# Attention values with the values stationary: two heads in the column halves, weights scaled before they are turned

## The chip, the cores and the metric

The kernel runs on one core of one Trainium2 chip. The metric is the device time of one execution, in microseconds; less is better. The engines are TensorE (PE in the rows; its weight loads are PEld), VectorE (DVE), ScalarE (ACT), GpSimd (POOL) and SyncE (SP), each with its own instruction queue, which it works off in order.

## What is computed

The reference is a small model of four layers on 512 tokens of width 1024, all in float32. Three of its layers hold an attention, and these are what the change is about. Cut to what matters:

```python
# layer 0, for each block of 128 queries, 8 heads of width 64 in 2 groups
o_cmp = masked_softmax(q @ kc.T * scale, cmask) @ vc      # 31 compressed keys
o_slc = masked_softmax(q @ ks.T * scale, smask) @ vs
o_win = masked_softmax(q @ kw.T * scale, wmask) @ vw
o = g0 * o_cmp + g1 * o_slc + g2 * o_win                  # gates per query and head
x = x + g_m * (concat(y_a, o) @ w_out)                    # y_a: a gated recurrence

# layer 1, 16 heads; every query keeps the keys that an index score picks
o = masked_softmax(q @ kg.T * scale, mask) @ vg
x = x + g_m * (o @ w_out)

# layer 3, 16 heads, a mask of dilated distances, rotary q and k
x = x + softmax(q @ k.T * scale + mask) @ v @ w_o
```

A row of weights is divided by its sum, and in layer 0 multiplied by its gate. That factor can be applied to the outputs (64 numbers a query and head) or to the weights (up to 512 a query and head); the result is the same.

## The kernel before

Activations lie turned: 128 features on the partitions, the 512 tokens along the row, eight such blocks for the width of 1024. A projection is worked off in "panels" of 128 output features. For each, SP loads 512 KB of raw weights, ACT rounds them to `w_hi` (L1160), POOL takes the difference `w_lo` (L578), and PE makes three matmuls a block, `three` (L606 to L609). Four panels are in flight (`RING`); POOL's work is nothing but these differences, in the order of the panels, and 26 additions in layer 2.

The three attentions (`attention(run, ...)`, one such function on PE, one on ACT, one on DVE, run = 0, 1, 2) share one scheme. The work is 32 pairs, and a pair is one block `i` of 128 queries with two heads `b` = 0, 1; its rows are `w = 128 * (i + 1)` keys wide. The order of the pairs is `PAIRS0` or `PAIRS1`: 16 pairs that alternate `i` = 3 and 0, then 16 that alternate `i` = 2 and 1. In what follows a **round** is two neighbouring pairs, so that an attention is 8 rounds of (3, 0) and 8 rounds of (2, 1). For pair `n`:

- PE `scores(n)`: two matmuls, one a head, of 64 rows each (L782), into the banks 0, 1 and 6 in turn;
- DVE `masked(n, b)`: adds the mask, writes the row to `prob` and its extreme to `stat` (L1732); `prob` holds two pairs;
- ACT: the exponential in place, and its sum (L1274);
- PE `turn(n)`: turns the rows, 128 columns a transpose (L792), into banks 2 and 3;
- ACT `copy_even(n)` (L1248) and DVE `copy_odd(n)` (L1742; for some pairs ACT, L1251) copy them to `probT`;
- PE `values(n)`: the turned weights are the stationary operand (128 by 128), 64 columns of values move; tokens come out on the partitions (L804), head `b` in columns `64 b`;
- DVE `invert(n)` (L1747) and `output(n)`: the reciprocal, in run 0 the gate (L1757), and the product into `orow` (L1764 in run 0, where it adds to what is there; L1767).

At the end blocks of `orow` are turned back to features on the partitions: PE `turn_out` (L817), ACT `out_high` (L1263) and DVE `out_low` (L1776), at hand-written places (`TURNED_AT`). `out_part` then makes the first two panels of the output projection, in two pieces.

The order on PE is `scores(n + 1)`, `turn(n)`, `values(n - 1)`; on DVE `masked(n, 0)`, `masked(n, 1)`, `copy_odd(n - 1)`, `invert(n - 1)`, `output(n - 2)`. Beside them DVE does other things: in run 0 `sum_in_steps` (24 steps, L1857 and L1860, on a 1 MB load each eight) and pieces of the recurrence, in run 1 `pick`, the choice of keys for the blocks still to come (L2154, L2156).

Two other places are touched. At the start, PE sums the squares of x over eight blocks (L861 to L865), and the norm of layer 0 waits for it (`invert_root(0)`, then `sum_first` and `first_h` on DVE, L1936 to L1944). Before the first attention, the compressed branch has its own values, `compressed_values` (L940) and `compressed_out` (L2054), which write `orow`.

## Time and profile before

| | us |
|---|---|
| median of 3 runs | 2536.79 |
| lowest, highest | 2529.05, 2537.76 |
| the profiled execution, its own time | 2536.1 |
| its span, first to last instruction | 2534.3 |
| PE, DVE, ACT, POOL busy in it | 2460.3, 1348.8, 935.5, 954.5 |
| mean granted TensorE clock | 0.981 |

Of the span, 1.8 us less than the execution's own time, PE is busy 97%. A busy PE is not a PE at its peak: matmuls are pipelined, and the duration of one record is longer than the time until the next can start. So steps are measured here from start to start. Times in rows are from the start of the span.

### The profile page before, as it was taken

What the parts mean: (1) busy time and instruction counts of PE and PEld (TensorE: products, weight loads), DVE (VectorE), ACT (ScalarE), POOL (GpSimd) and SP (SyncE); (2) the same over time, 40 slices, a digit from 0 to 9 for tenths busy, and PEclk for the clock granted to TensorE, in tenths of its full rate; (3) what the DMA queues carried; (4) which work ended last, traced back from release to release, by engine and by line L of the source; (5) the groups of instructions that cost most, each with busy time, mean ns of one, the idle gap of its engine ahead of it and who ended that gap; (6) DMA issues with size and microseconds to landing.
All of it is one profiled execution on the core that took longest, in us unless ns stands there. A gap on an engine that the chain in (4) does not pass through costs nothing.

```text
span 2534.3 us, 35767 instructions
## 1 busy us (share of the span) xinstructions
PE 2460.3 (97%) x12245; PEld 2025.4 (80%) x12245; DVE 1348.8 (53%) x2459; ACT 935.5 (37%) x1515; POOL 954.5 (38%) x409
## 2 busy tenths in 40 slices
PE   8999989999999899999999989999999999999998
PEld 7786778888877677888888768888888978888887
DVE  6777664443157765111117976545467465545445
ACT  3355433222233453322235444322246364432222
POOL 1320134444443103444444734444454402344443
PEclk9998999999999899999999999999999999999999
DMA  7540245554322102323323213333233201232322
GB/s 300 202 145 26 84 141 190 182 183 159 99 95 72 34 26 67 113 94 99 100 91 96 79 44 129 102 96 101 86 116 100 92 18 42 83 108 91 107 92 75
DMA packets 64344, 263.68 MB, mean 104 GB/s; under 512 B 7265, under 2 KB 7777, under 8 KB 57953
## 3 DMA queue, kind: packets, MB, share of 16 engines
q1 hardware_dynamic: 61056, 251.00, 29.9%
q10 hardware_dynamic: 3168, 11.08, 1.2%
q8 instruction: 76, 1.25, 0.2%
q14 instruction: 44, 0.35, 0.0%
HBM read 259.95 MB, written 2.10 MB: 103 GB/s over the span
## 4 chain that ended last, share of the span: by engine, by line
PE 85%; DVE 6%; issue 3%; ACT 2%; DMA 1%; DVEq 1%; POOLq 1%; POOL 1%; ACTq 0%; SPq 0%
PE bank L607 25%; PE bank L609 25%; PE bank L608 25%; PE bank L804 3%; PE bank L782 2%; PE bank L792 2%; DVE bank L1834 1%; DVE acc L1550 1%; DMA modraw<-in_pairs 1%; POOL w_lo L578 1%; POOLq L600 1%; DVE bank L2209 1%; PE bank L864 1%; PE bank L628 0%; PE bank L729 0%
## 5 line engine op out<-in xcount | busy, mean ns | idle before, releaser
L578 POOL TENSOR_TENSOR w_lo<-raw,w_hi 128x1024 fp32r<-128x1024 f32 x378 | 918.1, 2436 | 1548.2 <-ACT w_hi L1160 1546.8
L607 PE MATMUL bank<-h_hi,w_hi 128*128 128x512 f32 x1760 | 697.8, 396 | 12.6 <-DVE h_lo L1597 7.8
L608 PE MATMUL bank<-h_lo,w_hi 128*128 128x512 f32 x1760 | 690.3, 392 | 0.0
L609 PE MATMUL bank<-h_hi,w_lo 128*128 128x512 f32 x1760 | 690.1, 392 | 0.0
L1160 ACT ACTIVATE w_hi<-raw 128x1024 fp32r<-128x1024 f32 x378 | 392.6, 1051 | 472.9 <-PE bank L609 470.1
L607 PE MATMUL bank<-g_hi,w_hi 128*128 128x512 f32 x1072 | 418.6, 390 | 0.0
L609 PE MATMUL bank<-g_hi,w_lo 128*128 128x512 f32 x1072 | 417.2, 389 | 0.0
L608 PE MATMUL bank<-g_lo,w_hi 128*128 128x512 f32 x1072 | 417.1, 389 | 0.0
L607 PEld LDWEIGHTS bank<-h_hi,w_hi 128*128 128x128 f32 x1760 | 333.6, 190 | 89.9 <-DVE h_lo L1597 8.7
L609 PEld LDWEIGHTS bank<-h_hi,w_lo 128*128 128x128 f32 x1760 | 333.6, 190 | 71.2
L608 PEld LDWEIGHTS bank<-h_lo,w_hi 128*128 128x128 f32 x1760 | 333.9, 190 | 68.6 <-issue 0.5
L609 PEld LDWEIGHTS bank<-g_hi,w_lo 128*128 128x128 f32 x1072 | 201.2, 188 | 42.1
L608 PEld LDWEIGHTS bank<-g_lo,w_hi 128*128 128x128 f32 x1072 | 201.3, 188 | 41.5
L607 PEld LDWEIGHTS bank<-g_hi,w_hi 128*128 128x128 f32 x1072 | 201.3, 188 | 41.4
L1687 DVE TENSOR_TENSOR prod<-silu,bank 128x512 f32<-128x512 f32 x44 | 30.2, 687 | 299.8 <-PE bank L609 299.5
L1225 ACT ACTIVATE g_hi<-prod 128x512 f32 x66 | 41.7, 632 | 300.9 <-DVE prod L1687 197.3
L1613 DVE SCALAR_TENSOR_TENSOR x<-bank,plain,x 128x512 f32<-128x512 f32 x64 | 47.6, 749 | 153.7 <-PE bank L609 153.6
L1834 DVE SCALAR_TENSOR_TENSOR bank<-modraw,csil,bank 128x256 f32<-128x256 f32 x222 | 108.5, 489 | 17.2 <-issue 1.0
L1274 ACT ACTIVATE prob<-prob,stat 128x512 f32<-128x512 f32 (+1 forms) x192 | 105.6, 552 | 28.1 <-DVE stat L1732 28.0
L1613 DVE SCALAR_TENSOR_TENSOR x<-bank,modv,x 128x512 f32<-128x512 f32 x64 | 47.6, 749 | 112.1 <-PE bank L609 111.3
L1732 DVE CUSTOM_DVE_ANT_0 prob<-bank,mask 128x512 f32<-128x512 f32 (+1 forms) x192 | 86.4, 488 | 24.8 <-PE bank L782 21.5
L792 PEld LDWEIGHTS bank<-ident,prob 128*128 128x128 f32 x480 | 55.0, 149 | 51.7 <-ACT prob L1274 35.5
(300 smaller groups left out, 2685.8 us busy)
## 6 DMA issues: line engine op xcount, KB each, us to landing
raw<-in_panels SPq DMA_DIRECT2D x378, 512.0 KB, 3.5
modraw<-in_pairs SPq DMA_DIRECT2D x40, 1024.0 KB, 5.7
first_mods<-in_first SPq DMA_DIRECT2D x4, 2048.0 KB, 21.6
w<-in_w ACTq DMA_DIRECT2D x2, 2048.0 KB, 8.5
x<-in_x SPq DMA_DIRECT2D x1, 2048.0 KB, 8.6
out<-yout ACTq DMA_DIRECT2D x8, 256.0 KB, 2.2
mask<-in_causal ACTq DMA_DIRECT2D x1, 1024.0 KB, 4.8
mask<-in_dilated ACTq DMA_DIRECT2D x1, 1024.0 KB, 8.3
```

The source lines that it names most:

```text
L578: pool.tensor_tensor(w_lo[:, slot, :], raw[:, slot, :], w_hi[:, slot, :].bitcast(F32), ALU.subtract)\
L607: pe.matmul(out, w_h, m_h, start=start, stop=False)
L608: pe.matmul(out, w_h, m_l, start=False, stop=False)
L609: return pe.matmul(out, w_l, m_h, start=False, stop=stop)
L782: pe.matmul(bank[SBANK[(2 * n + b) % 3]][:, 0:w], q_of(run, pairs_[n], b), k_of(run, pairs_[n], b), start=True, stop=True).then_inc(score_ ...
L792: m = pe.transpose(bank[2 + b][:, P * j:P * j + P], prob[:, 2 * (n % 2) + b, P * j:P * j + P], ident[:, :])
L804: m = pe.matmul(bank[4 + n % 2][:, HD * b:HD * b + HD], probT[:, 2 * (n % 2) + b, P * j:P * j + P], v_of(run, pairs_[n], b, j), start=(j = ...
L1160: act.activation(w_hi[:, slot, :], raw[:, slot, :], ACT.Copy).then_inc(hi_ready, 1)
L1274: act.activation(row, row, ACT.Exp, bias=stat[:, 0, u % 64:u % 64 + 1], scale=-1.0, accum_out=stat[:, 1, u % 64:u % 64 + 1]).then_inc(exp_ ...
L1613: dve.scalar_tensor_tensor(out=x[:, n, :], in0=bank[p % RING][:, :], scalar=scale_by, in1=x[:, n, :], op0=MUL, op1=ADD).then_inc(bank_free, 1)
L1732: dve.tensor_tensor_reduce(prob[:, 2 * (n % 2) + b, 0:w], bank[SBANK[(2 * n + b) % 3]][:, 0:w], mask[:, i, 0:w], -SCALE, HIGHEST, ADD, ALU ...
L1834: m = dve.scalar_tensor_tensor(out=part if k < KB - 1 else to, in0=w[:, :, k, :], scalar=csil[:, k:k + 1], in1=part, op0=MUL, op1=ADD)
```

## The change

- **Values.** `values(n)` takes the values as the stationary operand (128 keys by 64 columns) and lets the turned weights move (128 tokens). The output is 64 features by 128 tokens, already the way the projection wants it; head 0 goes to partitions 0 to 63 and head 1 to 64 to 127 of the same bank, and the loop alternates the heads for each block of keys. The two pairs of a round, in run 0 four pairs (both branches), make a group that shares a bank, 4 or 5.
- **Scaling.** Tokens now lie along the row, so the factor of a token can't be applied to the outputs by a column. GpSimd multiplies the rows of weights by it, in place, before they are turned: 96 instructions on 128 by `2 w` elements. `turn(n)` waits for these (`weights_ready`), not for the exponentials.
- **Order.** The scores run three pairs ahead (`SCORES_AHEAD`), `prob` holds four pairs (`PROB_STEPS`), and the copies on ACT and DVE stand two steps later in their queues.
- **Gone.** `output`, `orow` and `turn_out`. `out_high` and `out_low` read a group's bank, 256 columns, 16 times in runs 1 and 2, 8 times in run 0. The first two output panels do seven of eight blocks before the last one.
- **Compressed branch.** Its probabilities are scaled by DVE (one instruction of 1024 columns), turned two panels later, and their values are two matmuls at the start of each group of run 0, in the same bank; `compressed_values` and `compressed_out` go.
- **Run 0's side work.** The sums for the modulation pause two steps after each eight (`STEP_AT`); the pieces `recurrence_low` go from DVE to POOL, between pairs 8 to 11.
- **Start.** POOL adds the squares two by two, so PE sums four blocks, not eight; `first_h(1)` stands before `sum_first(2)`, and PE does blocks 0 to 3 of the first panels ahead of `first_batch(2)`.

```diff
-        PAIRS0 = [(i, c, br) for both in TURNS for br in (1, 2) for c in range(4) for i in both]
+        PAIRS0 = [(i, c, br) for both in TURNS for c in range(4) for br in (1, 2) for i in both]
...
+        GROUP = (4, 2, 2)
...
         def odd_by_scalar(run, n):
-            return run == 0 and n % 2 == 1 or run == 1 and n < N_PAIR // 2
+            return run == 0 and n % 2 == 1 or run == 1 and n < N_PAIR // 2 and n % 2 == 0
...
         @block.gpsimd
+            def attention(run):
+                pairs_, at = (PAIRS0, PAIRS1, PAIRS1)[run], N_PAIR * run
+                for n in range(N_PAIR):
+                    w, u = P * (pairs_[n][0] + 1), 2 * (at + n) % 64
+                    both = prob[:, PROB_SLOT[n % PROB_STEPS], :, 0:w]
+                    pool.wait_ge(factor_ready, at + n + 1)
+                    pool.tensor_tensor(both, both, stat[:, 2, u:u + 2].rearrange("p (b o) -> p b o", o=1)
+                                       .broadcast_to((P, 2, w)), ALU.mult).then_inc(weights_ready, 1)
+                    if run == 0 and n in (8, 9, 10, 11):
+                        recurrence_low(n - 8)
...
+            for n in range(KB // 2):
+                pool.wait_ge(squares_ready, 2 * n + 2)
+                pool.tensor_tensor(sq0[:, 2 * n, :], sq0[:, 2 * n, :], sq0[:, 2 * n + 1, :], ALU.add).then_inc(two_added, 1)
+            split_from(0, P_OUT0 + RING)
+            attention(0)
...
         @block.tensor
                 def turn(n):
+                    pe.wait_ge(weights_ready, at + n + 1)
                     for b, copied in enumerate((pt_even, pt_odd)):
-                        pe.wait_ge(exp_ready, 2 * (at + n) + b + 1)
...
                 def values(n):
-                    if n >= 2:
-                        pe.wait_ge(o_done, at + n - 1)
...
-                            m = pe.matmul(bank[4 + n % 2][:, HD * b:HD * b + HD],
-                                          probT[:, 2 * (n % 2) + b, P * j:P * j + P], v_of(run, pairs_[n], b, j),
+                    if n % GROUP[run] == 0 and g >= 2:
+                        pe.wait_ge(ot_lo, OT_AT[run] + g - 1)
...
+                    for j in range(i + 1):
+                        for b in range(2):
+                            m = pe.matmul(out[rows_of(b), at_col:at_col + P], v_of(run, pairs_[n], b, j),
+                                          probT[:, 2 * (n % 2) + b, P * j:P * j + P], start=(run > 0 and j == 0),
...
                 for n in range(N_PAIR):
-                    if n + 1 < N_PAIR:
-                        scores(n + 1)
+                    if n + SCORES_AHEAD < N_PAIR:
+                        scores(n + SCORES_AHEAD)
                     turn(n)
                     if n:
                         values(n - 1)
...
         @block.scalar
                 for n, pair in enumerate(pairs_):
-                    if n:
-                        copy_even(n - 1)
+                    if n >= SCORES_AHEAD:
+                        copy_even(n - SCORES_AHEAD)
...
+                    if group_ended(run, n - SCORES_AHEAD - 1):
+                        out_high(n - SCORES_AHEAD - 1)
...
         @block.vector
                 for n in range(N_PAIR):
+                    masked(n, 0)
+                    if n >= SCORES_AHEAD and not odd_by_scalar(run, n - SCORES_AHEAD):
+                        copy_odd(n - SCORES_AHEAD)
+                    masked(n, 1)
                     if n:
                         invert(n - 1)
+                    if group_ended(run, n - SCORES_AHEAD - 1):
+                        out_low(n - SCORES_AHEAD - 1)
```

How this stands on the queues, at two places. First VectorE in the third attention, two neighbouring pairs of the first half. Before (the two ISA rows are `masked`, the numbers that follow are partitions by columns):

```order
L1732 ISA prob,stat<-bank,mask 128x128 [waits pt_done,score_ready]
L1732 ISA stat 128x1
L1732 ISA prob,stat<-bank,mask 128x128 [waits pt_done,score_ready]
L1732 ISA stat 128x1
L1742 COPY probT<-bank 128x512 [waits pv_done,pt_done]
L1747 RECIPROCAL stat<-stat 128x2 [waits exp_ready]
L1767 TENSOR_TENSOR orow_95<-bank,stat 128x128 [waits pv_done]
L1732 ISA prob,stat<-bank,mask 128x512 [waits pt_done,score_ready]
L1732 ISA stat 128x1
L1732 ISA prob,stat<-bank,mask 128x512 [waits pt_done,score_ready]
L1732 ISA stat 128x1
```

And now, the same two pairs' place in the queue:

```order
L1741 ISA prob,stat<-bank,mask 128x128 [waits pt_done,score_ready]
L1741 ISA stat 128x1
L1757 RECIPROCAL stat<-stat 128x2 [waits exp_ready]
L1769 TENSOR_TENSOR g_lo<-bank,g_hi 128x2x128 [waits ot_hi]
L1741 ISA prob,stat<-bank,mask 128x512 [waits pt_done,score_ready]
L1741 ISA stat 128x1
L1751 COPY probT<-bank 128x128 [waits pv_done,pt_done]
L1741 ISA prob,stat<-bank,mask 128x512 [waits pt_done,score_ready]
L1741 ISA stat 128x1
L1757 RECIPROCAL stat<-stat 128x2 [waits exp_ready]
L1741 ISA prob,stat<-bank,mask 128x128 [waits pt_done,score_ready]
L1741 ISA stat 128x1
```

The copy of a pair's odd head stood one step behind its `masked`; it stands three steps behind, between the two `masked` of a later pair, and the reciprocal of a pair comes after both `masked` of the next. The product into `orow` is gone.

Second TensorE in the same place. Before (L782 scores, L792 `turn`, L804 `values`):

```order
L792 MATMUL bank<-ident,prob 128x128 [waits pt_even,exp_ready]
L792 MATMUL bank<-ident,prob 128x128 [waits pt_odd,exp_ready]
L804 MATMUL bank<-v3t,probT 128x64 [waits pt_even,o_done]
L804 MATMUL bank<-v3t,probT 128x64 x3
L804 MATMUL bank<-v3t,probT 128x64 [waits pt_odd]
L804 MATMUL bank<-v3t,probT 128x64 x3
L782 MATMUL bank<-k_143,q_142 128x128 [waits masked_ready]
L782 MATMUL bank<-k_143,q_142 128x128
L792 MATMUL bank<-ident,prob 128x128 [waits pt_even,exp_ready]
L792 MATMUL bank<-ident,prob 128x128 x3
```

And now (L813 scores, L823 `turn`, L842 `values`):

```order
L823 MATMUL bank<-ident,prob 128x128 [waits pt_even,weights_ready]
L823 MATMUL bank<-ident,prob 128x128 [waits pt_odd]
L842 MATMUL bank<-probT,v3t 64x128 [waits pt_odd,pt_even]
L842 MATMUL bank<-probT,v3t 64x128 x7
L813 MATMUL bank<-k_141,q_140 128x128 [waits masked_ready]
L813 MATMUL bank<-k_141,q_140 128x128
L823 MATMUL bank<-ident,prob 128x128 [waits pt_even,weights_ready]
L823 MATMUL bank<-ident,prob 128x128 x3
L823 MATMUL bank<-ident,prob 128x128 [waits pt_odd]
L823 MATMUL bank<-ident,prob 128x128 x3
```

`turn` waits for `weights_ready`, which GpSimd gives, in the place of `exp_ready`; `values` needs one wait for both heads, and its rows have 128 moving columns and a 64-wide stationary operand.

## Rows read from the trace of the kernel before

**Rows 1.** The page: busy time, share of the span and instructions of TensorE.

```profile
PE 2460.3 (97%) x12245; PEld 2025.4 (80%) x12245; DVE 1348.8 (53%) x2459; ACT 935.5 (37%) x1515; POOL 954.5 (38%) x409
```

**Rows 2.** Windows: a stretch of the third attention, PE, PEld, DVE, ACT, POOL busy, clock.

```profile
2040.00:2070.00 30.00, 30.00 (x231) 23.92 (x230) 20.71 (x85) 18.94 (x62) 0.00 (x0) 1.00 0.01 2
```

**Rows 3.** Timeline: one round of the third attention's first half; start, us taken, engine, line.

```profile
2051.27 1.90 PE L804 MATMUL bank<-v3t,probT 128*128 128x64 f32 x16
...
2053.10 0.49 PE L782 MATMUL bank<-k,q 64*128 64x128 f32 x4
...
2053.52 1.09 PE L792 MATMUL bank<-ident,prob 128*128 128x128 f32 x8
...
2053.84 0.28 DVE L1732 CUSTOM_DVE_ANT_0 prob<-bank,mask 128x128 f32<-128x128 f32 x1
...
2054.65 0.69 DVE L1742 COPY probT<-bank 128x512 f32<-128x512 f32 x1 [0.52 <-PE bank L792]
...
2055.26 0.15 DVE L1747 RECIPROCAL stat<-stat 128x2 f32<-128x2 f32 x1
...
2056.27 1.90 PE L804 MATMUL bank<-v3t,probT 128*128 128x64 f32 x16
```

**Rows 4.** Timeline: one round of the third attention's second half.

```profile
2097.37 1.45 PE L804 MATMUL bank<-v3t,probT 128*128 128x64 f32 x12
...
2098.66 0.61 PE L817 MATMUL bank<-ident,orow 128*128 128x128 f32 x4
...
2102.81 1.45 PE L804 MATMUL bank<-v3t,probT 128*128 128x64 f32 x12
```

**Rows 5.** Timeline: matmuls whose stationary operand is 64 columns wide.

```profile
1464.61 1.09 PE L1097 MATMUL bank<-wsT,v2t 128*64 128x128 f32 x16
```

**Rows 6.** Groups and one line's durations (ns, min/median/max): GpSimd's tensor operations.

```profile
L578 POOL TENSOR_TENSOR w_lo<-raw,w_hi 128x1024 fp32r<-128x1024 f32 x378 | 918.1, 2436 | 1548.2 <-ACT w_hi L1160 1546.8 <-issue 1.1
L599 POOL TENSOR_TENSOR cout<-cout,tapped 128x512 f32<-128x512 f32 x26 | 35.1, 1351 | 5.1 <-issue 2.9 <-ACT tapped L1433 2.2
L578 POOL TENSOR_TENSOR w_lo<-raw,w_hi x378: 2334/2398/3092, 17.1 to 2505.8; 128x1024 fp32r<-128x1024 f32 x189
```

**Rows 7.** Timeline: the first exponential of each half, attentions one, two, three.

```profile
192.94 0.72 ACT L1274 ACTIVATE prob<-prob,stat 128x512 f32<-128x512 f32 x1
...
242.79 0.61 ACT L1274 ACTIVATE prob<-prob,stat 128x384 f32<-128x384 f32 x1 [0.49 <-DVE stat L1732]
...
841.20 0.72 ACT L1274 ACTIVATE prob<-prob,stat 128x512 f32<-128x512 f32 x1 [3.00 <-DVE stat L1732]
...
894.89 0.62 ACT L1274 ACTIVATE prob<-prob,stat 128x384 f32<-128x384 f32 x1
...
2031.41 0.72 ACT L1274 ACTIVATE prob<-prob,stat 128x512 f32<-128x512 f32 x1
...
2071.49 0.61 ACT L1274 ACTIVATE prob<-prob,stat 128x384 f32<-128x384 f32 x1
```

**Rows 8.** Windows: two stretches of the second attention, columns as in group 2.

```profile
841.20:865.10 23.90, 23.49 (x93) 17.37 (x94) 14.65 (x57) 11.29 (x34) 0.00 (x0) 0.50 0.05 18
...
872.00:888.00 16.00, 13.62 (x98) 9.94 (x97) 13.49 (x58) 11.31 (x34) 0.00 (x0) 1.00 0.01 2
```

**Rows 9.** Groups, 840 to 895 us: the picks beside the second attention, VectorE.

```profile
L2154 DVE MAX8 top<-iacc 128x8 f32<-128x256 f32 x16 | 6.7, 421 | 0.4
L2156 DVE MATCH_REPLACE8 iacc<-top,iacc 128x256 f32<-128x256 f32 x16 | 6.5, 409 | 0.0
```

**Rows 10.** Timeline: the kernel's first sums on TensorE and VectorE.

```profile
10.61 13.79 PE L864 MATMUL bank<-ones,sq 128*128 128x1 f32 x64 [10.61 <-ACT sq L1293]
...
24.83 0.18 DVE L1558 RECIPROCAL root<-root 128x4 f32<-128x4 f32 x1 [4.52 <-ACT root L1298]
```

**Rows 11.** Timeline: half of the compressed values on TensorE.

```profile
174.77 1.97 PE L942 MATMUL bank<-vdiag,cpT 128*128 128x256 f32 x8
```

**Rows 12.** Groups, 193 to 243 us: VectorE's sums of modulation weights, first attention.

```profile
L1860 DVE SCALAR_TENSOR_TENSOR modsum<-modraw,csil,modsum 128x256 f32<-128x256 f32 x10 | 4.8, 484 | 0.9
```

268 lines of the change are left out of this document (106 added, 162 removed).

## The prediction

> **What bounds the kernel now.** The page says TensorE: busy 97% of the span [rows 1]. That share is an average, and the change touches only the three attentions and two places near the start, so the windows and the timeline of those stages come next. In the third attention's steady stretch PE is busy all of the time at full clock, DVE 69%, ACT 63%, and GpSimd not at all [rows 2]. The timeline of one round (a pair of block 3 and one of block 0) shows PE going round without a gap: `values` of the big pair 1.90 us with its tail, scores of the small pair, eight transposes, `values` of the small pair, the next scores, and again after 5.00 us [rows 3]. Rounds of blocks 2 and 1 take 5.44 us, of which the transposes of finished outputs are 0.54 (from 2098.66 to the scores at 2099.20) [rows 4]. So here PE is the bound, and `values` is its dearest part: 20 records a round at 0.112 us, 2.2 of 5 us. The first halves of the other two attentions are slower: 49.9 us in the first (192.94 to 242.79) and 53.7 us in the second (841.20 to 894.89), against 40.1 us in the third [rows 7]. In the second, PE ran at its lower level, 1.2 GHz, for 24 us, with DVE busy only 61% of it [rows 8].
>
> **The change, term by term.** The sum is made against the profiled execution's own 2536.1 us, 0.7 under the median.
>
> *Values on PE.* The nearest rows are matmuls of the very shape in layer 2: 16 records, 64-wide stationary operand, 128 moving columns, alternating between the column halves, in 1.09 us against 1.90 us for 16 of today's [rows 5, 3]. Both have a tail of 0.27 us, so the new records come in pairs every 0.11 us. That is 0.05 us a record, 1.0 us a round. A round of blocks (3, 0) would need 5.00 - 1.01 = 3.99 us of PE, one of (2, 1) 5.44 - 1.01 - 0.54 = 3.89 us. Between scores and transposes of different shape PE already shows starts 0.2 us apart where neighbours of one shape need 0.11; two more such seams a pair, at 0 to 0.1 us each, make 4.0 to 4.4 us. The page TensorEngine Tiling (Array Packing) of the Trainium skill, Key Properties, says that a change of tiling mode drains the engine; by that the upper end would hold, the sum being some 5 us higher.
>
> *The GpSimd step.* 128 x 1024 with two inputs takes POOL 2.44 us in the mean (2.33 to 3.09), 128 x 512 1.35 us [rows 6]; the line through both gives 1.89 us for 768 and 0.81 us for 256. A round needs 3.25 us of POOL in either half: under 4, so its throughput is hidden. Its latency is not. DVE works in order, and the copy of pair n-2 stands ahead of the second `masked` of pair n+1, behind which stands the reciprocal of pair n, for which POOL waits, and PE for POOL. So there is a loop that closes once a round: transposes of the big pair to the copy's start 1.13 us (2053.52 to 2054.65), copy 0.61, `masked` of the small pair 0.28, reciprocal 0.15, scaling 2.44, two hand-overs of 0.04 (the copy starts 0.04 after the last transpose ends) [rows 3, 6]: **4.7 us**. With blocks (2, 1) the transposes are two fewer (0.22), copy and scaling three quarters: 0.91 + 0.48 + 0.4 + 0.15 + 1.89 + 0.1 = 3.9 us, level with PE. I take 4.7 for the first halves, 4.2 for the second.
>
> *Third attention.* First half 8 x 4.7 = 37.6 against 40.1; second 8 x 4.2 = 33.6 against 8 x 5.44 = 43.5. The pipeline must fill once: the first transpose waits for the second exponential, the reciprocal and the scaling, 0.9 + 0.15 + 2.44 + hand-overs, +4 us. That wait stands beside scores already made, and may leave PE cold a little longer, +2. At the end eight transposes at 0.11 go, -0.9. Sum: -2.5 - 9.9 + 4 + 2 - 0.9 = **-7**.
>
> *First attention.* The loop is longer by the gate's product (as a reciprocal, with its drain 0.2): 4.95 us. The four `recurrence_low` are 1.35 us each on POOL inside two rounds, which lengthens each by about 1.1 us. DVE also does 24 sums of 0.48 us [rows 12]; these fit in its slack in the first half, and in the second bring it near the pace, so 4.5 us there. The waits for the 1 MB loads of these weights, which the new pauses should hide, lie inside the old halves and are not counted apart. First half 8 x 4.95 + 2.2 + 2.7 for about 7 cold us = 44.5 against 49.9; second 36 against 43.5; fill +4.6 (a piece of the recurrence now precedes it); end -1.5. Sum **-10**. At the lower clock PE needs twice 4 us a round, which makes a cold microsecond cost 0.4.
>
> *Second attention.* In its first half DVE also picks keys: 16 picks of 256 columns at 0.42 + 0.41 and some 0.2 between, and five of 384 columns, scaled by the columns to 1.4, 23.5 us in all [rows 9]. DVE's own round there is 1.7 for `masked` (two of 0.61 as the copy of that width, two of 0.28 less a tail of 0.06), 0.2 for one copy, 0.3 for two reciprocals, and 0.4 for `out_low` (256 columns, between 0.28 and 0.69), so 8 x 2.6 + 23.5 = 44.5 us: DVE becomes the bound while PE is warm. Cold rounds (10 us of them, a guess between 0 and the 24 of today) add 4, waits in order 1: 49.5 against 53.7. Second half 33.6 against 43.5, plus 2 for the three pairs that DVE is ahead; the fill hides behind the picks. End -1. Sum **-13**.
>
> *Start.* PE's sums, 64 records in 13.79 us at the lower clock, hold back the reciprocal at 24.83, and with it DVE's further sums [rows 10]. Half the records save up to 6.9 us; DVE is free 4.5 us earlier (that is how long it waited), but then waits for its next weights, which come in one DMA queue behind others. Between 0 and 4.5, I take **-2.5**. *Compressed values:* two stretches like 1.97 us go from a PE without gaps [rows 11], **-3.9**; the matmuls that replace them stand in the first attention, where PE has slack.
>
> Total: -7 - 10 - 13 - 2.5 - 3.9 = -36.4, so about **2500 us**, 1.4% faster.
>
> Against the move speaks a rule of the Trainium skill. GPSIMD Engine Reference, section 1, says that GpSimd shares its SBUF interfaces with VectorE, with contention when VectorE has two SBUF inputs. Only the 24 sums of the first attention are of that kind [rows 12]; by the rule each could hold up POOL by 0.48 us, up to 12 us more, 2512 us. The row of 378 subtractions, with a maximum of 3.09 us over a median of 2.40 [rows 6], allows such delays but does not say whose they are. It is part of my case below, with 0.08 of its chance, since most of these sums fall where GpSimd has slack.
>
> **Rivals.**
> *PE sets the pace everywhere*, because the loop through DVE and GpSimd is shorter than I chained it. For it: the pieces are generous by tails; against it: they are in one queue order. Then the first halves of the first and third attention run at 4.1: 8 x 0.85 + 8 x 0.6 = 11.6 us less, and the start brings its 4.5: 2486 us.
> *The clock.* Each fill leaves PE idle for some 4 to 7 us, and before, in the second attention, a spell of 24 us at 1.2 GHz followed a shorter wait [rows 8]. If each attention has such a spell, 17 us more of cold at 0.4 in each: +20, 2520 us. [...]
> *GpSimd is slow at this.* The scaling reads a broadcast operand and writes in place, which no row shows. Every microsecond x on 1024 columns lengthens the loop by 8x in each of the first halves of runs 0 and 2 (from its own slack on in run 1), by 0.75x in 24 further rounds, and the fills by 3x: 37x to 45x. At x = 0.4 nothing but 20 us is left; at x = 0.9 (3.3 us, the row's maximum being 3.09) the gain is gone, and from x = 1.2 (3.6 us) on the kernel is over 0.5% **slower**. A POOL at 4 us a scaling gives about 2565 us.
> *It doesn't do what it says:* the column halves run one after the other. Then a record costs 0.107 and nothing is gained in `values`; rounds would stay at 4.9 to 5, with fills on top: 2530 us. Rows 5 speak plainly against it.
>
> **How the numbers follow.** My case 0.50; PE sets the pace 0.18; the clock 0.14; a somewhat slow GpSimd or serial halves, ending between 2524 and 2549, 0.10; a GpSimd beyond 3.6 us, 0.05; the rest, 0.03, below 2478. The unknown ends inside my case (seams 0 to 5, start -2 to +2.5, cold spells 0 to +8, DVE waits) span 2488 to 2514. With the clock's case to 2520 and PE's to 2486 and their own spread, the range is 2479 to 2525. Half a percent, 12.7 us, is what a measurement of this kernel can tell from no change: faster than 2524 has 0.86, the same 0.09, slower 0.05.
>
> **What would show it.** Right: `values` of the big pair in 1.1 us; rounds of 4.6 to 4.9 us in the third attention's first half with PE waiting for the POOL scaling once a round, and 4.0 to 4.3 in the second half; scalings of about 2.4 us; about 4 us between the first scores and the first transpose more than before; a reciprocal near 21 us. Wrong: scalings over 3 us, a PE without waits at the first halves, spells of 1.2 GHz of over 10 us in the first and third attention, or copies that wait for something else than transposes.

## The result and the profile after

The changed kernel takes **2514.3 us** (median of 4 runs, 2513.2 to 2515.5) against 2537.1 us for the kernel before in the same comparison: a ratio of 0.9915, 95% interval 0.9903 to 0.9927. That is 22.7 us or 0.9% faster. The forecast was 2500 us, 36 us faster, with a range of 2479 to 2525 us: the sign and the range held, the gain was two thirds of what was worked out.

The page of the changed kernel, whose span is 2513.0 us; the line answers to [rows 1]:

```profile
PE 2407.1 (96%) x12149; PEld 1946.9 (77%) x12149; DVE 1334.2 (53%) x2348; ACT 937.8 (37%) x1523; POOL 1085.3 (43%) x513
```

TensorE has 53 us less work and a span that is 21.3 us shorter. The other 32 us have become waiting. Where, is read off six marks on TensorE: the first scores of each attention, and the first matmul of the projection behind it. Before (timeline; start, us taken, engine, line):

```profile
189.71 0.70 PE L782 MATMUL bank<-ksT,q 64*128 64x512 f32 x2 [1.11 <-DVE vtok L1537]
288.00 0.48 PE L607 MATMUL bank<-h_hi,w_hi 128*128 128x512 f32 x1
836.54 0.70 PE L782 MATMUL bank<-k,q 64*128 64x512 f32 x2 [0.78 <-DVE k L1526]
938.65 0.48 PE L607 MATMUL bank<-h_hi,w_hi 128*128 128x512 f32 x1
2029.38 0.70 PE L782 MATMUL bank<-k,q 64*128 64x512 f32 x2 [1.38 <-DVE v3t L1540]
2115.24 0.48 PE L607 MATMUL bank<-g_hi,w_hi 128*128 128x512 f32 x1
```

After:

```profile
187.05 0.70 PE L813 MATMUL bank<-ksT,q 64*128 64x512 f32 x2 [2.20 <-DVE vtok L1546]
283.92 0.50 PE L638 MATMUL bank<-h_hi,w_hi 128*128 128x512 f32 x1
831.38 0.70 PE L813 MATMUL bank<-k,q 64*128 64x512 f32 x2 [0.78 <-DVE k L1535]
925.32 0.50 PE L638 MATMUL bank<-h_hi,w_hi 128*128 128x512 f32 x1
2019.51 0.70 PE L813 MATMUL bank<-k,q 64*128 64x512 f32 x2 [1.38 <-DVE v3t L1549]
2095.23 0.50 PE L638 MATMUL bank<-g_hi,w_hi 128*128 128x512 f32 x1
```

| stretch | before | after | change | forecast |
|---|---|---|---|---|
| up to the first attention | 189.7 | 187.1 | -2.7 | -6.4 |
| first attention | 98.3 | 96.9 | **-1.4** | -10 |
| first to second | 548.5 | 547.5 | -1.1 | 0 |
| second attention | 102.1 | 93.9 | -8.2 | -13 |
| second to third | 1090.7 | 1094.2 | +3.5 | 0 |
| third attention | 85.9 | 75.7 | **-10.1** | -7 |
| behind it | 419.1 | 417.8 | -1.3 | 0 |

These sum to -21.3 us, the difference of the two spans (2534.3 and 2513.0). So the third attention gave more than forecast, the first next to nothing, and 3.5 us went in a stretch that the change doesn't touch. The first mark itself moves by over 1 us without cause in the program: in nine kernels of this study that are the same up to there it lies between 185.7 and 187.1 us.

**Third attention.** One round of its first half on TensorE, as in [rows 3], with GpSimd's scaling and the low half of a group that falls in it (timeline):

```profile
2044.06 0.49 PE L813 MATMUL bank<-k,q 64*128 64x128 f32 x4
2044.48 1.09 PE L823 MATMUL bank<-ident,prob 128*128 128x128 f32 x8
2045.51 0.44 PE L842 MATMUL bank<-probT,v3t 128*64 128x128 f32 x4
2045.88 1.13 PE L813 MATMUL bank<-k,q 64*128 64x512 f32 x4
2046.67 1.89 POOL L599 TENSOR_TENSOR prob<-prob,stat 128x1024 f32<-128x1024 f32 x1 [1.08 <-DVE stat L1757]
2046.94 0.44 PE L823 MATMUL bank<-ident,prob 128*128 128x128 f32 x2
2046.95 0.36 ACT L1270 ACTIVATE g_hi<-bank 128x256 fp32r<-128x256 f32 x1
2047.30 1.09 PE L842 MATMUL bank<-probT,v3t 128*64 128x128 f32 x16
2047.34 0.42 DVE L1769 TENSOR_TENSOR g_lo<-bank,g_hi 128x256 fp32r<-128x256 f32 x1 [0.75 <-ACT g_hi L1270]
2047.68 0.68 DVE L1741 CUSTOM_DVE_ANT_0 prob<-bank,mask 128x512 f32<-128x512 f32 x1
2048.43 0.49 PE L813 MATMUL bank<-k,q 64*128 64x128 f32 x4
```

The 16 records of the big pair take 1.09 us where they took 1.90 [rows 3], exactly the time of layer 2's rows of that shape [rows 5]. Scores to scores are 4.37 us (2044.06 to 2048.43). In a round TensorE waits some 0.1 us only: the last matmul of `values` starts 0.30 us before the scores, where 0.20 us is the step at the other changes of shape. The loop through VectorE and GpSimd, 4.7 us in the forecast, is shorter because the scaling is. By form, between 2020 and 2090 us:

```profile
L599 POOL TENSOR_TENSOR prob<-prob,stat 128x1024 f32<-128x1024 f32 x8 | 15.1, 1893 | 9.6 <-DVE stat L1757 9.6
L582 POOL TENSOR_TENSOR w_lo<-raw,w_hi 128x1024 fp32r<-128x1024 f32 x2 | 4.7, 2356 | 6.8 <-ACT w_hi L1168 6.8
```

A scaling takes 1.89 us for 1024 columns (1.47, 1.04 and 0.61 us for 768, 512 and 256), where the forecast took the 2.44 of the weights' subtraction [rows 6], whose rows here still take 2.36.

**First attention.** TensorE's costliest wait between 187 and 285 us (in total, times, longest):

```profile
PE bank L813 <- DVE stat L1741: 18.6, 21, 2.5
```

And all executions of the side sums behind the first of each chain (duration in ns, min/median/max):

```profile
L1847 DVE SCALAR_TENSOR_TENSOR modsum<-modraw,csil,modsum x21: 686/1308/2160, 204.8 to 279.9; 128x256 f32<-128x256 f32 x21
```

TensorE waits 18.6 us for masks, 21 times. And the sums, 484 ns before [rows 12], take 1308 ns in the median and up to 2160. VectorE waits 7.2 us, in 8 times, for ScalarE's high halves of the outputs besides. The timeline shows what they stand beside:

```profile
270.00 1.04 POOL L599 TENSOR_TENSOR prob<-prob,stat 128x512 f32<-128x512 f32 x1 [1.63 <-DVE stat L1762]
270.01 1.31 DVE L1847 SCALAR_TENSOR_TENSOR modsum<-modraw,csil,modsum 128x256 f32<-128x256 f32 x1
272.86 1.47 POOL L599 TENSOR_TENSOR prob<-prob,stat 128x768 f32<-128x768 f32 x1 [1.83 <-DVE stat L1762]
272.87 1.74 DVE L1847 SCALAR_TENSOR_TENSOR modsum<-modraw,csil,modsum 128x256 f32<-128x256 f32 x1
```

Each of the two begins with a scaling (10 ns apart) and ends 0.27 us behind its end: 1.04 and 1.31, 1.47 and 1.74. So it is with all 21: every one ends 0.28 us behind the end of a scaling, 15 began within 0.03 us of its start, and the other six while one was running. A sum reads two operands from SBUF. A mask reads one from PSUM and one from SBUF, and the mask at 2047.68 above takes its usual 0.68 us within a scaling (2046.67 to 48.56). The scalings beside sums are no longer than others.

This was to be seen before the change, in both directions. Timeline of the kernel before, VectorE's additions of squares (two SBUF inputs; 34 of its 59 began with no GpSimd instruction at work and took 0.69 us) and GpSimd's subtractions (2.40 us in the median):

```profile
957.40 2.40 POOL L578 TENSOR_TENSOR w_lo<-raw,w_hi 128x1024 fp32r<-128x1024 f32 x1 [3.04 <-ACT w_hi L1160]
957.93 2.42 DVE L1550 TENSOR_TENSOR acc<-acc,sq 128x512 f32<-128x512 f32 x1 [0.98 <-ACT sq L1170]
...
1345.57 4.20 DVE L1550 TENSOR_TENSOR acc<-acc,sq 128x512 f32<-128x512 f32 x2
1346.40 2.82 POOL L578 TENSOR_TENSOR w_lo<-raw,w_hi 128x1024 fp32r<-128x1024 f32 x1
```

The addition at 957.93 began second and took 2.42 us. The subtraction at 1346.40 began while an addition was running and took 2.82 us, and the next addition, begun within that subtraction, was held in its turn. So in these rows the engine that begins second is the one that waits. The 25 additions that began beside a GpSimd instruction at work took 1.24 to 2.87 us, and all 48 subtractions over 2.45 us began while VectorE was at an instruction with no operand in PSUM.

### The profile page after: what moved, and what is told of

It reads as the page before. It is cut to its first block, busy times and chain, and to the rows that moved or that the text cites. A ratio compares the mean times of both kernels' runs of the same rounds, so it can differ in the third digit from the quotient of the medians.

```text
span 2513.0 us, 35279 instructions
## 1 busy us (share of the span) xinstructions
PE 2407.1 (96%) x12149; PEld 1946.9 (77%) x12149; DVE 1334.2 (53%) x2348; ACT 937.8 (37%) x1523; POOL 1085.3 (43%) x513
## 4 chain that ended last, share of the span: by engine, by line
PE 57%; issue 22%; POOL 9%; DVE 5%; ACT 2%; DVEq 2%; POOLq 1%; DMA 1%; SPq 0%; ACTq 0%
PE bank L638 17%; PE bank L640 17%; PE bank L639 17%; POOL w_lo L582 9%; PE bank L823 2%; PE bank L813 1%; DVEq L1761 1%; PE bank L842 1%; DVE acc L1559 1%; ACT prob L1282 1%; POOLq L629 1%; DVE bank L2177 1%; DVE prob L1741 1%; PE bank L760 0%; PE bank L659 0%
## 5 line engine op out<-in xcount | busy, mean ns | idle before, releaser
L599 POOL TENSOR_TENSOR prob<-prob,stat 128x1024 f32<-128x1024 f32 (+1 forms) x96 | 120.4, 1255 | 123.2 <-DVE stat L1757 77.4
L1670 DVE TENSOR_TENSOR bank<-bank,rb 128x512 f32<-128x512 f32 x88 | 61.4, 698 | 63.7 <-PE bank L640 52.1
```

The costliest lines, as they stand in the source:

```text
L599: pool.tensor_tensor(both, both, stat[:, 2, u:u + 2].rearrange("p (b o) -> p b o", o=1) .broadcast_to((P, 2, w)), ALU.mult).then_inc(weigh ...
L1670: dve.tensor_tensor(bank[slot][:, :], bank[slot][:, :], rb[:, :], MUL)
```

## The experiments

The theory to test: in the first attention, VectorE is held by GpSimd's running scaling whenever it has two SBUF inputs; in the second, VectorE's order with its picks sets the pace; in the third, TensorE does. The start brings next to nothing. Rivals stand in each expectation. All edits are to the changed kernel. The kernel before, run beside each group of them, had medians of 2535.0 to 2537.5 us. The first scores of the second attention come at 831.38 us in the changed kernel and at 829.76 in one whose program is the same up to there, so stretches between marks are compared, not only totals.

### Side sums in PSUM

```diff
+                part = MODBANK[:, 2 * P:4 * P].rearrange("p (n m) -> p n m", m=P)
...
-                    dve.tensor_scalar(to, w, csil[:, 0:1], None, MUL)
+                    dve.tensor_scalar(part, w, csil[:, 0:1], None, MUL)
...
-                    last = dve.scalar_tensor_tensor(out=to, in0=w, scalar=csil[:, k:k + 1], in1=to, op0=MUL, op1=ADD)
+                    last = dve.scalar_tensor_tensor(out=to if k == KB - 1 else part, in0=w, scalar=csil[:, k:k + 1],
+                                                    in1=part, op0=MUL, op1=ADD)
```

> The changed kernel with one edit: the 24 side sums of the first attention keep their running sum in a free part of PSUM bank 7 and write SBUF only at the last of eight steps, so each VectorE sum reads one SBUF operand instead of two (the pair of small matmuls that uses the first sum moves from pair 15 to pair 12, since it writes the same bank). Theory A (VectorE, with two SBUF inputs, is held until GpSimd's running scaling ends; 21 sums took 1.31 us in the median instead of 0.48): the sums fall to about 0.5 us, rounds of the first attention fall from 5.96 to about 4.6 us, its two halves from 45.5 and 42.6 us to about 40 and 35; the kernel 10 to 16 us under the changed one, about 2501 us. Theory B (the two engines' instructions only overlap by chance; what lengthens the rounds is the amount of VectorE's work): the time stays within 3 us of 2514. Theory C (any SBUF read of VectorE is held while GpSimd runs): sums still over 1 us, 2514.

Measured: **2501.2 us** (ratio to before 0.987, interval 0.9854 to 0.9887), 13.1 us under the changed kernel. The sums:

```profile
L1848 DVE SCALAR_TENSOR_TENSOR bank<-modraw,csil,bank x18: 487/490/490, 204.6 to 263.2; 128x256 f32<-128x256 f32 x18
L1848 DVE SCALAR_TENSOR_TENSOR modsum<-modraw,csil,bank x3: 480/481/481, 220.4 to 266.7; 128x256 f32<-128x256 f32 x3
```

TensorE's wait for masks in that attention:

```profile
PE bank L813 <- DVE stat L1741: 6.9, 8, 2.5
```

The sums take 490 ns at the most, the waits fall from 18.6 to 6.9 us, and the attention takes 84.8 us between its marks (185.74 to 270.49) instead of 96.9. The work is the same and GpSimd scales as before. The last sum of each chain (the second row) still writes SBUF, and all still read the weights there, yet none is held: it is the second SBUF input that costs. Theories B and C fall. Of the 13.1 us, 12.1 lie in this attention.

### Most of the sums left out

```diff
-                else:
+                elif k == KB - 1:
```

> The changed kernel without steps 1 to 6 of each of the three weighted sums beside the first attention (18 of the 24 instructions are left out, so these weights are wrong). Theory A (held sums set the rounds of 5.96 us): the 18 sums go with their drains, and rounds without one run at 3.7 to 4.5 us: the first attention's halves about 38 and 34 us, 13 to 19 us under the changed kernel, about 2498 us. Theory B (the pace of the first attention is set by the loop through scaling and recurrence, the sums sit in slack): less than 4 us change.

Measured: 2496.4 us in one run, 17.9 less, within theory A's 13 to 19. The first attention takes 84.1 us between its marks (186.56 to 270.67), 12.8 less than in the changed kernel; 4.4 of the other 5.1 us lie in the stretch from the second attention to the third, on which see below. Without the sums the first attention is only 0.7 us shorter than with sums in PSUM. So unheld sums are nearly free here, as the forecast had it ("these fit in its slack").

### The scaling twice

```diff
-                    pool.tensor_tensor(both, both, stat[:, 2, u:u + 2].rearrange("p (b o) -> p b o", o=1)
-                                       .broadcast_to((P, 2, w)), ALU.mult).then_inc(weights_ready, 1)
+                    for time in range(2):
+                        m = pool.tensor_tensor(both, both, stat[:, 2, u:u + 2].rearrange("p (b o) -> p b o", o=1)
+                                               .broadcast_to((P, 2, w)), ALU.mult)
+                        if time == 0:
+                            pool.drain()
+                    m.then_inc(weights_ready, 1)
```

> The changed kernel with each of GpSimd's 96 scalings issued twice, a drain between (the weights come out wrong). The scaling takes 1.89 us for a pair of block 3 and 0.62 us for one of block 0, 1.47 and 1.04 for blocks 2 and 1. Theory A (TensorE sets the third attention's rounds of 4.37 and 4.33 us, and the loop through VectorE and GpSimd has a slack of some 0.3 us in the first half and of about 1 us in the second): first-half rounds rise to about 5.9 us (4.1 of loop and 1.9), so 35.5 us becomes 47; second-half rounds to about 5.0 (GpSimd's own work 5.0 us a round); 25 to 35 us more over the three attentions with the first one's held sums, about 2545 us. Theory B (with three pairs of scores ahead the latency of the scaling is covered by other pairs, and only GpSimd's throughput counts): rounds of 5.0 us in either half of the third attention, some 12 to 16 us more over all, about 2528 us.

Measured: 2560.1 us in one run, 45.8 more, above either theory. The third attention takes 101.3 us instead of 75.7 (2039.54 to 2140.86). Of TensorE's waits there the greatest is now

```profile
PE bank L827 <- POOL prob L600: 15.4, 13, 2.0
```

and windows of two stretches, one in either half (busy time of PE, PEld, DVE, ACT, POOL, then the granted clock), read

```profile
2045.00:2090.00 45.00, 35.02 (x258) 21.43 (x260) 21.11 (x90) 24.98 (x76) 34.87 (x29) 0.84 0.04 13
2097.00:2128.00 31.00, 26.68 (x234) 16.47 (x234) 18.35 (x78) 22.00 (x67) 29.29 (x25) 1.00 0.00 1
```

Theory A is the nearer one: first-half rounds were 5.9 to 7.6 us (5.9 expected), second-half rounds 5.21 (5.0). In the first half GpSimd is busy only 77% of the time (34.87 of 45 us), so it is the latency of the scaling that counts, and theory B falls; in the second it is busy 94% and sets the pace by throughput. What neither theory had is the clock: TensorE's new pauses brought it down to a mean of 0.84 in the first of the two stretches. This also prices the rival of a slow GpSimd: 1.89 us more on 1024 columns costs 45.8 us, 24 us for each microsecond, where the prediction had 37 to 45. (The marks put 12.7, 8.9 and 25.6 us of it in the three attentions; in the first the longer scalings also held the sums.) The prediction had no slack for the loop against TensorE in the first halves, and in the second halves it counted 0.75x a round; there 2.5 us more of scaling lengthened the round by 0.88 us only (4.33 to 5.21).

### One head after the other

```diff
-                    for j in range(i + 1):
-                        for b in range(2):
+                    for b in range(2):
+                        for j in range(i + 1):
```

> The changed kernel with the two loops of the values exchanged: all blocks of the first head, then all of the second, so that neighbours share a column half. Theory A (two heads in the two column halves run at the same time, 0.11 us a pair of records, while two in the same half follow each other at 0.107 to 0.11 each): the values of a big pair take 1.9 instead of 1.0 us, rounds of the third attention 4.9 to 5.3 instead of 4.35 us; 48 rounds by 0.6 to 0.9 us where TensorE sets the pace, 20 to 35 us more, about 2540 us. Theory B (the gain over before comes from the stages that went away, not from the halves running together): within 5 us of 2514.

Measured: 2526.0 us in one run, 11.7 more. But 6.0 of these stand before the first edited instruction: TensorE waited 1.6 us at 136.4 us, ran at the lower clock for some 10 us behind it, and began the first scores at 193.01 us. So the marks decide here too. The third attention is 5.1 us longer (2026.21 to 2107.05), the second 1.5 us, the first 98.2 us where kernels with its order unchanged show 96.9 to 98.0. The same piece as above:

```profile
2056.86 1.58 PE L842 MATMUL bank<-probT,v3t 128*64 128x128 f32 x16
```

1.58 us is between 1.09 and the 1.9 expected. Single records show why: the first head's first four matmuls start 0.11 us apart, then come eight starts some 0.05 us apart, which read as two rows of 0.11 us side by side, and the last four are alone again. (The records don't name the head.) So the column halves run together in part even when the program lists one behind the other. Theory A holds in kind, as two heads in step are quicker, but not in size: third-attention rounds are 4.75 and 4.54 us (from 4.37 and 4.33), not 4.9 to 5.3. The loop order is worth 0.5 us a big pair, and the rest of the 0.81 us saved against before is had in either order.

### The old start, and the pause cut in two

The first kernel takes the squares over eight blocks on TensorE again, with both engines' old order. The second keeps the new squares and edits TensorE's order alone:

```diff
-            by_k(0, h_hi, h_lo, 0, (0, 1, 2, 3))
+            by_k(0, h_hi, h_lo, 0, (0, 1))
             first_batch(2)
+            by_k(0, h_hi, h_lo, 0, (2, 3))
             first_batch(3)
```

> The changed kernel with the start as before: TensorE's sums of squares over all eight blocks, VectorE and TensorE in the old order of first parts. Theory A (the new start gives next to nothing: its earlier reciprocal, 21.11 us against 24.83, is met by a wait for the second weights at 23.24 and by a spell of 1.2 GHz of 10 us behind TensorE's new pause; the first panels end at 61.81 us against 62.31): 0 to +1 us, 2514 to 2515. Theory B (it gives what was forecast): +2.5, 2517.

> The changed kernel, start alone edited: TensorE's matmuls for parts 2 and 3 stand again behind the third batch of sums, so that its pause is cut in two. Theory A (the low spell at 46.3 us comes from the pause of TensorE between 42.4 and 50.6 us and costs some 2.8 us): with work at 44 to 49 us the third row of matmuls runs at 2.4 GHz from its start at 50.6, first panels end near 59.5 us, 2 to 3 us less, 2511.5. Theory B (TensorE's pause only moves to 37 to 44 us and brings its low spell there): 0 to +2 us.

Measured: 2516.0 us (2515.4 to 2516.3) and 2516.7 us (2515.9 to 2517.3), 1.6 and 2.3 us more than the changed kernel's 2514.3. The rows of the changed kernel that answer to [rows 10]:

```profile
12.25 6.95 PE L887 MATMUL bank<-ones,sq 128*128 128x1 f32 x32 [12.25 <-POOL sq L612]
21.11 0.18 DVE L1567 RECIPROCAL root<-root 128x4 f32<-128x4 f32 x1 [1.00 <-ACT root L1308]
23.24 0.62 DVE L1816 TENSOR_SCALAR bank<-first_mods,csil 128x384 f32<-128x384 f32 x1 [1.95 <-DMA first_mods<-in_first]
```

The window from 45 to 62 us, of the changed kernel:

```profile
45.00:62.00 17.00, 14.69 (x60) 12.36 (x61) 13.82 (x28) 4.41 (x6) 0.51 (x1) 0.70 0.44 154
```

Of the second kernel:

```profile
45.00:62.00 17.00, 17.00 (x85) 14.10 (x85) 13.38 (x28) 4.77 (x6) 3.27 (x2) 0.96 0.46 162
```

The squares take 6.95 us instead of 13.79, the reciprocal comes 3.7 us earlier, and VectorE then waits 1.95 us for its next weights. Between 42.2 and 50.4 us TensorE has waits and matmuls of one column only, and from 46.1 to 56.3 us its clock is at the lower level, 1.2 GHz (mean 0.70 in the window shown). With the pause cut in two the mean is 0.96 and the first panels end at 59.3 us instead of 61.8, as expected. Yet the first attention's scores come no earlier: at 188.47 us, 1.4 us behind the changed kernel's and behind all of the nine with its start (185.7 to 187.1). Two of TensorE's waits between 60 and 189 us:

```profile
PE bank L919 <- DVE blocks L1973: 2.4, 1, 2.4
PE bank L659 <- DVE modsum L1822: 2.1, 1, 2.1
```

TensorE, ahead by 2.5 us, waits 4.5 us for VectorE's next sums and blocks, which the changed kernel had waits of 0.7 us for. VectorE bounds what follows the start, so what TensorE gains there doesn't last; why the scores come later still isn't shown. Neither theory fits the total of 2.3 us more; it is nearest to B's 0 to 2. The old start reaches the first scores at 186.80 us, 0.25 us earlier than the changed kernel and within the spread of its start; its total is 1.6 us higher, between the two theories. So the new start is worth between nothing and 1.6 us; the runs don't settle it further.

### Low halves of the recurrence back on VectorE

```diff
-                    if run == 0 and n in (8, 9, 10, 11):
-                        recurrence_low(n - 8)
```

and the same call, with its subtraction, in VectorE's loop.

> The changed kernel with the four low halves of the recurrence (128 x 512, 1.40 us each on GpSimd) back on VectorE, behind the first head's mask of the same pairs. Theory A (each stands in the loop of its pair on GpSimd, 1.1 us in the forecast, while on VectorE it costs 0.7 us of an engine that is 80% busy there; two SBUF inputs, so it will be held until a running scaling ends and take 1 to 2 us): nothing to gain, -1 to +3 us, 2513 to 2517. Theory B (GpSimd's order is what lengthens the first half): 3 us less, 2511.

Measured: 2512.0 us (2510.9 to 2512.9), 2.4 us less: outside theory A's 2513 to 2517 and near theory B's 2511. Yet theory B is not what happened. The marks decide: the first attention takes 100.4 us, 96.9 in the changed kernel's profile and 97.8 to 98.2 in five others whose first attention has its sums and scalings unchanged, while the untouched stretch to the third attention is 1089.9 us instead of 1094.2. So where the edit acts it costs 2 to 3.5 us, against theory B, and the total came down in a stretch that the edit doesn't touch. On VectorE the four took 678 ns each: they stood behind masks and were not held, as theory A had expected.

**The untouched stretch.** From the second attention's end to the third's first scores the thirteen profiles of this study show 1089.8 to 1091.4 us in five kernels (the kernel before and this one among them) and 1093.4 to 1095.0 us in eight (the changed kernel among them), though no edit acts there. The traces show where they part: at the same collision, in layer 2. The changed kernel (timeline):

```profile
1318.15 2.39 POOL L582 TENSOR_TENSOR w_lo<-raw,w_hi 128x1024 fp32r<-128x1024 f32 x1 [1.66 <-ACT w_hi L1168]
1318.29 2.81 DVE L1559 TENSOR_TENSOR acc<-acc,sq 128x512 f32<-128x512 f32 x1 [0.46 <-issue]
```

The kernel of this section:

```profile
1319.22 1.48 DVE L1557 TENSOR_TENSOR acc<-acc,sq 128x512 f32<-128x512 f32 x2
1320.07 2.90 POOL L582 TENSOR_TENSOR w_lo<-raw,w_hi 128x1024 fp32r<-128x1024 f32 x1 [1.68 <-ACT w_hi L1166]
```

In all eight long kernels VectorE's second addition begins 0.11 to 0.14 us behind the subtraction and takes 2.8 us; in all five short ones it begins 0.06 to 0.25 us ahead of it and takes 0.69 us. And in the eight alone TensorE then waits twice, for 1.1 us each (1344.16 and 1352.39 us in the changed kernel). No run changed this order by itself, so that the rest follows from it is argued; part of it lies in the clock (mean 0.86 from 1341 to 1365 us in the changed kernel, 0.93 in the same piece here). It is 3.5 of the 13.7 us that the forecast missed. The runs of any one changed kernel lie within 2.4 us of each other, so this goes with the kernel: totals of two kernels compare no finer than about 4 us.

### VectorE's low half one pair later

```diff
-                    if group_ended(run, n - SCORES_AHEAD - 1):
-                        out_low(n - SCORES_AHEAD - 1)
+                    if group_ended(run, n - SCORES_AHEAD - 2):
+                        out_low(n - SCORES_AHEAD - 2)
...
-                    if group_ended(run, n - 1):
-                        out_low(n - 1)
+                    if group_ended(run, n - 2):
+                        out_low(n - 2)
```

> The changed kernel with VectorE's low half of a finished group moved one pair later (it waited 6.7 us in all for ScalarE's high half in the second attention's first half, 7.0 us in the first attention). Theory A (VectorE bounds the second attention's first half, busy 86% with these waits as most of the rest, and is near the bound in the first): 4 to 6 us less there and up to 3 in the first attention, 2506 to 2510. Theory B (the loop through masks, exponentials, scaling and copies bounds it, the waits lie in slack): within 2 us of 2514.

Measured: **2505.9 us** (2504.6 to 2506.4), 8.4 us less: theory A, a little beyond its size. Second attention 86.5 us between its marks instead of 93.9 (830.72 to 917.20), third 73.9 instead of 75.7, first no shorter (97.9). VectorE's greatest wait in the second attention's first half, in the changed kernel:

```profile
DVE h_lo L1769 <- ACT h_hi L1270: 6.7, 6, 1.6
```

In this one:

```profile
DVE prob L1741 <- PE bank L813: 1.9, 5, 0.7
```

Six waits for ScalarE's high half, 6.7 us, are gone, and the half is 6.8 us shorter (44.1 us from the first exponential to the next half's): here a wait on the engine that bounds was lost one for one. In the third attention, too, the 0.1 us of waiting before the scores was this: the mask at 2047.68 stood behind the low half at 2047.34; the round is now 4.27 us.

### The picks left out

```diff
-            attention(1, pick if picks else None, len(picks))
+            attention(1, None, 0)
```

> The changed kernel without the 21 picks of keys that stand beside the second attention (0.8 to 1.1 us of VectorE each, 22 to 23 us in all; the masks of its blocks 1 and 2 stay unpicked, so its output is another). Theory A (VectorE's order, picks in it, is the bound of that first half): its 51 us fall to 38 to 40, the pace of TensorE with its pauses and some cold rounds, 11 to 13 us less over all, about 2502 us. Theory B (the loop through scaling and exponentials sets it, the picks sit in slack): under 4 us less.

Measured: 2497.0 us in one run, 17.4 less, of which 4 are the untouched stretch. The second attention takes 80.7 us (829.76 to 910.47) instead of 93.9, so 13.2 less: theory A. Its first half is 37.9 us instead of 51.0.

### Both edits, and one more

> The changed kernel with two edits together: running sums of the first attention in PSUM, and VectorE's low half of a group one pair later in all three attentions. Apart they gave 13.1 and 8.4 us. Theory A (they act in different places: held sums in the first attention, waits for ScalarE in the second, where VectorE is the bound): 21 to 24 us under the changed kernel, with 1 to 3 us more in the first attention, whose VectorE still waited for ScalarE with the sums made short: about 2491 us. Theory B (with the sums short the first attention is at TensorE's pace and the rest is given back to other waits or to spells at 1.2 GHz): 2495 or more.

Measured: **2489.7 us** (2488.9 to 2490.8), 24.6 us under the changed kernel; 21.5 were the sum of the two alone: theory A. The first attention takes 82.8 us between its marks, 2.0 less than with the sums in PSUM alone, as theory A had it.

```diff
-            return run == 0 and n % 2 == 1 or run == 1 and n < N_PAIR // 2 and n % 2 == 0
+            return run == 0 and n % 2 == 1 or run == 1 and n < N_PAIR // 2
```

> The kernel of both edits, and ScalarE also copies the second head's turned weights of the small pairs in the second attention's first half (eight copies of 128 x 128, 0.29 us each on VectorE there). Theory A (VectorE is the bound of that half): 2 us less than without this edit. Theory B (after the waits for ScalarE went, it is the loop of copies, masks and scaling that sets the half, and a copy behind the exponentials in ScalarE's order comes later): 0 to 2 us more.

Measured: **2484.4 us** (2483.5 to 2485.7), ratio to before 0.9796, interval 0.9777 to 0.9816: 53 us or 2% faster than before, 1.2% faster than the changed kernel. Of the 5.3 us under the kernel before it, 1.2 are in the second attention (85.3 us against 86.5), the sign of theory A at 0.6 of its size; 3.1 are the untouched stretch, in which this kernel is one of the five short ones.

## Why the prediction was right, and where it was off

- **What bounds** was right for the third attention, and so was the price of the new values: 1.09 us for 16 records, as in the row of layer 2. The total, 2514.3 us, lies at the slow end of the forecast's own case (2488 to 2514), but by errors of both signs: 3.7, 8.6 and 4.8 us too hopeful up to and in the first and in the second attention, 3.1 us too careful in the third, and 3.5 us in a stretch that it didn't count.
- **The GpSimd step** was mis-sized: "128 x 1024 with two inputs takes POOL 2.44 us" is the price of a subtraction of two full operands. A scaling by a broadcast factor took 1.89 us, so by the same chain the loop is 4.1 us and not 4.7 (an estimate), and TensorE set the pace at 4.37 (first half) and 4.33 us (second). This was the rival *PE sets the pace everywhere* for this stage, and a sign of being wrong, "a PE without waits at the first halves", came nearly as written in the third attention; "rounds of 4.6 to 4.9 us" and "scalings of about 2.4 us" didn't. The shorter rounds are 2.6 us of the first half. The 4.0 to 4.4 us for a round with its seams held: starts are 0.20 us apart at a change of shape. The Trainium skill's TensorEngine Tiling (Array Packing), Key Properties, has a change of tiling mode drain the engine. The timeline agrees, and with the upper end of the seams: the step from the last transpose to `values`, 0.11 us before, is 0.20 us now that its operand is 64 columns wide.
- **First attention** is where the forecast failed: "DVE also does 24 sums of 0.48 us [rows 12]; these fit in its slack". 21 of them have two SBUF inputs and met a scaling; they took 1.31 us in the median, 16 us more than before in all. The prediction weighed such a collision, by the Trainium skill's GPSIMD Engine Reference, section 1, but in the other direction, GpSimd held by VectorE for 0.48 us each, and gave it 0.08. The two do contend when VectorE has two SBUF inputs, as that section says, and the row of 378 subtractions, which "does not say whose they are", was answered by the additions of squares in the same trace: the one that begins second waits, and here that was VectorE. That "up to 12 us more, 2512" came out at 13.1 us in the first experiment is luck, since the 12 were 24 waits of GpSimd. "Most of these sums fall where GpSimd has slack" was the wrong reason: a sum stands behind the reciprocal that releases the scaling, so in 15 of 21 the two start together by the program's order. Nor were they the only ones of that kind: two of the recurrence's products (`ya`, 0.69 us before) took 1.33 and 2.43 us.
- **Second attention.** "DVE becomes the bound" was right, shown by two experiments. Its first half took 51.0 us (836.04 to 887.01, the exponentials that answer to [rows 7]) against 49.5: the sum had "waits in order 1" where VectorE waited 6.7 us for ScalarE's high halves, and 4 us for cold rounds, which was ample: with those waits gone the half takes 44.1 us, what the forecast had without any cold rounds. From there to the projection it took 38.3 us (887.01 to 925.32), where 33.6 + 2 - 1 = 34.6 was forecast: VectorE stops three pairs earlier than TensorE, and those are emptied at the end.
- **The fill** came at the size that was forecast: in the third attention the first transpose is 6.4 us behind the first scores where it was 2.9, 3.5 us more for "+4". But it was put at the wrong end of the first and third. Measured from exponential to exponential, the third's first half had no +4 and +2 in it (35.5 us, 2021.54 to 2057.01, even with the first round, against 43.6 forecast); the second half to the projection took 38.2 us where 33.6 - 0.9 were forecast. The two errors, -8.1 and +5.5, cancel in part, which is luck, and what is left of them is most of the 3 us by which that attention did better. In the first attention, too, the first half came out shorter, 45.5 us against 44.5 + 4.6 forecast with the fill, and the whole miss lies in the second, 48.1 us to the projection (235.82 to 283.92) against 45.2 before and 36.2 forecast: there most rounds with a held sum took 5.96 us, and with the sums in PSUM rounds took 4.0 to 5.1.
- **Start and compressed values.** "Between 0 and 4.5, I take -2.5" ended near its lower bound; that VectorE bounds what follows is the reason as far as is known. The reciprocal came at 21.11 us, as forecast. With the old start the first scores are at 186.80, 2.9 us earlier than in the kernel before (189.71), against 3.9 forecast for the compressed values.
- **The clock.** The second attention again begins at the lower level (windows):

```profile
831.00:851.00 20.00, 12.66 (x62) 6.81 (x62) 17.70 (x60) 11.01 (x27) 7.36 (x5) 0.66 0.12 41
871.00:887.00 16.00, 10.90 (x98) 6.78 (x98) 11.78 (x52) 9.79 (x31) 6.79 (x5) 1.00 0.01 2
```

The mean is 0.66 in the first 20 us and full from 871 on. Over the whole of the three attentions it is 0.95, 0.91 and 0.95, where it was 0.93, 0.88 and 0.98 before: less time at the lower level in the first two, 3 us more of it in the third. The rival of 17 us more in each attention fell. Between 40 and 62 us the spell of 3.4 us at the lower level became one of 10.2 (46.1 to 56.3 us), which was not forecast.

## What to carry over

An operation that is moved to GpSimd has two prices: its own, to be taken from a row with the same kind of operands, and what it and VectorE's instructions with two SBUF inputs do to each other, since the one that begins second waits for the other. Both can be looked up in the trace before the change, in the rows whose duration is far from their own median. Look at which engine's instruction releases the other: an accumulation put right behind the release begins together with it, and lost here each time. Keep running sums in PSUM there. And on an engine near the bound, ask for each wait on a third engine whether it could stand one step later, before counting slack.

## What was unexpected of the hardware

VectorE's `scalar_tensor_tensor` with both tensors in SBUF (128 x 256) took 0.48 us alone and GpSimd's remaining time plus 0.28 us beside it (1.31 and 1.74 us); with one of them in PSUM 0.49 us beside the same GpSimd work. It goes the other way where VectorE begins first: a subtraction of 2.40 us took up to 2.90 us behind an addition. Which of the two began first, by 0.1 to 0.3 us, went with 3 us or more of a stretch of 1090. GpSimd's scaling by a broadcast operand cost 1.89 us where its subtraction of two full operands cost 2.36. And matmuls on different column halves overlapped across several places of the queue, also when the program had all of one half first (16 records in 1.58 us; 1.09 in alternation).
